# A value product turned round in the attention of a two-layer encoder: f32 probabilities as weights, and another order on TensorE

## The reference

```python
def block(args):                      # one block of 128 queries
    s = einsum('bqhd,bkhd->bhqk', qn_b, k_nope) + einsum('bqhd,bkd->bhqk', qr_b, k_rope)
    p = jax.nn.softmax(s * scale, axis=-1)
    return einsum('bhqk,bkhd->bqhd', p, val)      # 8 heads, val: 64 columns a head
...
mod = (silu(c) @ w_mod[l] + b_mod[l])             # six rows of 1024 a layer and group
h = rmsnorm(x) * (1 + sc1) + sh1
m = concat(rmsnorm(attn), rmsnorm(sgu)) @ w_out   # attn from the blocks above
x = x + ga1 * rmsnorm(m)
h = rmsnorm(x) * (1 + sc2) + sh2
x = x + ga2 * rmsnorm((silu(h @ w_gate) * (h @ w_up)) @ w_down)
```

## Time and profile before

| what | value |
|---|---|
| median of 3 runs | 3696.1 us (3693.67 to 3696.79) |
| the profiled execution's own time | 3700.85 us |
| its span | 3699.0 us |
| mean granted TensorE clock | 0.958 of full speed |
| PE busy | 3358.4 us, 91% of the span, 19532 matmul records |
| DVE, ACT, POOL busy | 1582.8, 1031.7, 1395.8 us |

### The profile page before, as it was taken

One profiled execution on the slowest core, in us unless ns is written; L12 is line 12 of the kernel. 1 busy time (PEld: TensorE's weight loads), 2 busy tenths in 40 slices (PEclk: granted clock), 3 DMA queues, 4 the chain that ended last, 5 costly groups with the idle time before them and its releaser, 6 DMA issues. The chain is left out here.

```text
span 3699.0 us, 48829 instructions
## 1 busy us (share of the span) xinstructions
PE 3358.4 (91%) x19532; PEld 3024.3 (82%) x19532; DVE 1582.8 (43%) x2807; ACT 1031.7 (28%) x2298; POOL 1395.8 (38%) x804
## 2 busy tenths in 40 slices
PE   5997888879899999999998978887989999999996
PEld 1987677767799998889988867776779999899996
DVE  3115677774333333533233146877333333352223
ACT  2323454563300101211004234776330010121001
POOL 2210577740454444545540302000045444455441
PEclk7998899989999999999999989998999999999998
DMA  6204544433322223322223134111232222233221
GB/s 206 70 21 145 150 137 132 155 101 86 115 79 75 75 69 84 113 83 75 80 65 104 58 116 133 27 37 61 75 114 79 76 75 69 83 123 92 80 75 63
DMA packets 397728, 337.90 MB, mean 91 GB/s; under 512 B 107192, under 2 KB 325000, under 8 KB 397504
## 3 DMA queue, kind: packets, MB, share of 16 engines
q1 hardware_dynamic: 249808, 233.18, 20.6%
q10 hardware_dynamic: 147696, 101.61, 9.4%
HBM read 282.87 MB, written 51.87 MB: 90 GB/s over the span
## 5 line engine op out<-in xcount | busy, mean ns | idle before, releaser
L580 POOL TENSOR_SCALAR w_hi<-raw 128x1024 fp32r<-128x1024 f32 (+2 forms) x400 | 436.8, 1092 | 2194.4 <-PE ps L597 2045.4
L582 POOL TENSOR_TENSOR w_lo<-raw,w_hi 128x1024 fp32r<-128x1024 f32 (+2 forms) x400 | 966.7, 2417 | 33.3
L595 PE MATMUL ps<-ht_lo,w_hi 128*128 128x320 f32 x2816 | 874.1, 310 | 5.2 <-DVE ht_lo L1358 3.2
L596 PE MATMUL ps<-ht_hi,w_lo 128*128 128x320 f32 x2816 | 872.2, 310 | 0.0
L597 PE MATMUL ps<-ht_hi,w_hi 128*128 128x320 f32 x2816 | 872.2, 310 | 0.0
L595 PE MATMUL ps<-w_lo,ht_hi 128*128 128x512 f32 (+2 forms) x2040 | 783.8, 384 | 59.4 <-DVE ht_lo L1358 24.3
L596 PE MATMUL ps<-w_hi,ht_lo 128*128 128x512 f32 (+2 forms) x2040 | 777.5, 381 | 0.0
L597 PE MATMUL ps<-w_hi,ht_hi 128*128 128x512 f32 (+2 forms) x2040 | 775.6, 380 | 0.0
L595 PEld LDWEIGHTS ps<-ht_lo,w_hi 128*128 128x128 f32 x2816 | 530.6, 188 | 8.1 <-DVE ht_lo L1358 3.9
L596 PEld LDWEIGHTS ps<-ht_hi,w_lo 128*128 128x128 f32 x2816 | 530.7, 188 | 1.6
L597 PEld LDWEIGHTS ps<-ht_hi,w_hi 128*128 128x128 f32 x2816 | 530.5, 188 | 0.0
(11 more groups left out here) (127 smaller groups left out, 3710.7 us busy)
## 6 DMA issues: line engine op xcount, KB each, us to landing
raw<-in_w_gate_dram SPq DMA_DIRECT2D x88, 512.0 KB, 3.8
raw<-in_w_up_dram SPq DMA_DIRECT2D x88, 512.0 KB, 3.8
raw<-in_w_down_dram SPq DMA_DIRECT2D x88, 512.0 KB, 3.5
raw<-in_w_mod_dram SPq DMA_DIRECT2D x80, 512.0 KB, 4.1
x_rows<-tokm ACTq DMA_DIRECT2D x30, 512.0 KB, 5.0
x_old<-x_rows ACTq DMA_DIRECT2D x30, 512.0 KB, 4.3
kv_rows<-stage ACTq DMA_DIRECT2D x20, 512.0 KB, 3.3
tokm<-kv_rows ACTq DMA_DIRECT2D x30, 320.0 KB, 4.1
```

What stands on the lines that cost most here:

```text
L580: pool.tensor_scalar(hi, r, 1.0, 0.0, ALU.mult, ALU.add).then_inc(s_whi, 1)
L582: pool.tensor_tensor(lo, r, hi.bitcast(F32), ALU.subtract).then_inc(s_w, 1)
L595: pe.matmul(out, lhs[0], rhs[1], start=first, stop=False)
L596: pe.matmul(out, lhs[1], rhs[0], start=False, stop=False)
```

## The change

The value product is turned round: the turned probabilities, now one f32 buffer a unit without hi and lo, are the weights, V in f32 is the moving operand with 64 columns, and the result comes out with queries on the partitions, so nothing is turned back. `probs_hi`, `probs_lo`, `v_hi`, `v_lo`, `values_copy`, `transpose_values`, `low_half` and `invert_sums` go. Of the turned probabilities of a prompt unit ACT copies the first four tiles and DVE the last four; a sample unit is copied by one of them. DVE scales a unit's 64 columns by the inverse of its sum. The buffers `gate_row` and `x_old` hold the turned probabilities during attention. V has two buffers, loaded for two heads at the start.

PE's step is scores of unit n, transposes of unit n-1, value product of unit n-2, with the `prep` transposes between; the loop has two steps beyond the units instead of four. The modulation products stand at every odd step, the last at step 79, at the end of the step, and wait until DVE has read the value product that stands just before them on PE out of bank 6.

```diff
-        def pT(b): return [f[:, 4 * TOK + 2048 * b:...].rearrange("p (k q) -> p k q", q=256) for f in hf]
+        pT = [x.rearrange("p (k q) -> p k q", q=P) for x in (gate_row[:, :], x_old[:, :, :].rearrange("p h c -> p (h c)"))]
...
+        PT_ACT = [s < 2 * NBLK - 1 for s in range(NU)]
+        PT_DVE = [s != 2 * NBLK - 2 for s in range(NU)]
...
-        MOD_WITHIN, MOD_END = {}, {}
...
+        MOD_AT = {2 * i + 1: i for i in range(NLH)}
...
# SP
-                sp.wait_ge(s_vl, 2 * H * (l + 1))
+                sp.wait_ge(s_pv, unit_no(l, H - 1, 0))
                 for t in range(4, NT - 1):
                     sp.dma_start(tokm[:, 1, t, :], sgu_d[t]).then_inc(s_sld[0], 16)
-                sp.wait_ge(s_pt, NPT * H * (l + 1))
+                sp.dma_start(tokm[:, 1, NT - 1, :], sgu_d[NT - 1]).then_inc(s_sld[2], 16)
+                sp.wait_ge(s_pta, act_copies(l + 1, 0, 0))
+                sp.wait_ge(s_ptd, dve_copies(l + 1, 0, 0))
                 for t in range(4):
                     sp.dma_start(tokm[:, 1, t, :], sgu_d[t]).then_inc(s_sld[1], 16)
...
# PE
                     if h or i >= 8:
                         pe.wait_ge(s_htl, transposed[0])
-                        if transposed[1]:
-                            pe.wait_ge(s_od, transposed[1])
...
-                    v = v_prm(h % 2) if k0 == 0 else v_smp
-                    hi, lo = pT(n % 2)
-                    for k in range(part * nk // 2, (part + 1) * nk // 2):
-                        pe.matmul(ps[:, 6, 0:256], v[:, k, :], lo[:, k, :], start=k == 0, stop=False)
-                        ins = pe.matmul(ps[:, 6, 0:256], v[:, k, :], hi[:, k, :], start=False, stop=k == nk - 1)
...
+                    pe.wait_ge(s_pca, act_copies(l, h, s + 1))
+                    pe.wait_ge(s_pcd, dve_copies(l, h, s + 1))
+                    if u:
+                        pe.wait_ge(s_od, u)
+                    if modulated[0]:
+                        pe.wait_ge(s_mrow, modulated[0])
+                    for k in range(nk):
+                        ins = pe.matmul(ps[:, 6, 0:VD], pT[u % 2][:, k, :], v_rows[h % 2][:, k0 + k, :], start=k == 0, stop=k == nk - 1)
...
-                def modulation(i, blocks):
+                def modulation(i, units):
-                    pe.wait_ge(s_ot, blocks)
+                    if units:
+                        pe.wait_ge(s_od, units)
...
-                for n in range(NS + 4):
+                for n in range(NS + 2):
                     if n < NS:
                         scores(*STEPS[n])
+                    if 1 <= n <= NS:
+                        transpose_probs(*STEPS[n - 1])
...
+                    if n >= 2:
+                        values(*STEPS[n - 2])
...
+                    if l == 0 and n in MOD_AT:
+                        modulation(MOD_AT[n], n - 1)
...
# ACT and DVE
+                        act.activation(pT[u % 2][:, 0:w, :], ps[:, 4, 0:w * P].rearrange("p (k q) -> p k q", q=P), ACT.Copy).then_inc(s_pca, 1)
...
+                        dve.tensor_copy(pT[u % 2][:, k0:k0 + w, :], ps[:, 5, 0:w * P].rearrange("p (k q) -> p k q", q=P)).then_inc(s_pcd, 1)
...
+                    link(dve.reciprocal(c, c))
+                    dve.wait_ge(s_pv, u + 1)
+                    dve.tensor_scalar(tokm[:, 0, BLKS[b][2] + i, h * VD:(h + 1) * VD], ps[:, 6, 0:VD], c, None, ALU.mult).then_inc(s_od, 1)
...
-                    link(dve.tensor_tensor(rows, ps[0:2, 6, 256:512], tbank[...], ALU.add))
                     dve.wait_ge(s_ml, i + 1)
-                    dve.tensor_tensor(rows, rows, stage[...], ALU.add).then_inc(s_mrow, 1)
+                    prod = ps[0:2, 6, 256:512]
+                    link(dve.tensor_tensor(prod, prod, tbank[...], ALU.add))
+                    dve.tensor_tensor(rows, prod, stage[...], ALU.add).then_inc(s_mrow, 1)
```

More of the change, by code:

```diff
@@ L333, in trunk_program @@
         NU = len(UNITS)
-        PTB = [-(-BLKS[b][1] // 4) for b, _ in UNITS]
-        NPT = sum(PTB)
+        PT_ACT = [s < 2 * NBLK - 1 for s in range(NU)]
+        PT_DVE = [s != 2 * NBLK - 2 for s in range(NU)]
+        NPA, NPD = sum(PT_ACT), sum(PT_DVE)
         STEPS = [(h, s) for h in range(H) for s in range(NU)]
@@ L418, in trunk_program @@
         s_hl = sem("head_loaded")
-        s_hv = sem("v_loaded")
+        s_hv = [sem(f"v_loaded{i}") for i in range(2)]
         s_prep = sem("head_transposed")
@@ L456, in trunk_program, with unit_no, act_copies, dve_copies @@
         DPP = 2 * HT_
+        def unit_no(l, h, s): return (l * H + h) * NU + s
+        def act_copies(l, h, s):
+            return (l * H + h) * NPA + sum(PT_ACT[:s])
+        def dve_copies(l, h, s): return (l * H + h) * NPD + sum(PT_DVE[:s])
         def after_product(eng, key):
@@ L677, in _ @@
                             ins.then_inc(rdy[b], 1)
[L680 removed]
+                transposed = [l * H * NPREP]
                 def prep(h, i):
@@ L716, in transpose_probs @@
                 def transpose_probs(h, s):
-                    u = (l * H + h) * NU + s
+                    u = unit_no(l, h, s)
                     pe.wait_ge(s_exp, u + 1)
-                    n = (l * H + h) * NPT + sum(PTB[:s])
-                    nk = BLKS[UNITS[s][0]][1]
-                    before = PTB[s - 1] if s else PTB[-1]
-                    for c in range(PTB[s]):
-                        if n:
-                            pe.wait_ge(s_ptl, n - before + 1 if c == 0 and before == 2 else n)
-                        for j in range(min(4, nk)):
-                            ins = pe.transpose(ps[:, 4 + c, j * P:(j + 1) * P], p_buf[u % 2][:, (4 * c + j) * P:(4 * c + j + 1) * P], ident[:, :])
-                        ins.then_inc(s_pt, 1)
@@ L749, in _ @@
-                modulated = [0]
-                def transpose_values(h, b):
-                    n = (l * H + h) * NBLK + b
-                    pe.wait_ge(s_ot, n + 1)
-                    if n:
-                        pe.wait_ge(s_od, n)
-                    pe.wait_ge(s_htl, transposed[0])
-                    transposed[1] += 1
-                    for i in range(2):
-                        ins = pe.transpose(ps[:, 7, o_place(i):o_place(i) + P], ot_buf[n % 2][:, i * P:(i + 1) * P], ident[:, :])
-                    ins.then_inc(s_tr, 1)
@@ L762, in modulation, with four @@
-                def modulation(i, blocks):
+                    w = min(4, BLKS[UNITS[s][0]][1])
+                    def four(bank, k0):
+                        for j in range(w):
+                            ins = pe.transpose(ps[:, bank, j * P:(j + 1) * P], p_buf[u % 2][:, (k0 + j) * P:(k0 + j + 1) * P], ident[:, :])
+                        return ins
+                    if PT_ACT[s]:
+                        if act_copies(l, h, s):
+                            pe.wait_ge(s_pca, act_copies(l, h, s))
+                        four(4, 0).then_inc(s_pta, 1)
@@ L800, in _ @@
                         prep(*prep_at(n, PREP_LATE))
-                    if l == 0 and n in MOD_END:
-                        modulation(MOD_END[n], (n - 2) // 2)
+                    if l == 0 and n in MOD_AT:
+                        modulation(MOD_AT[n], n - 1)
                 def transpose_ffn(key):
@@ L1132, in exponentials @@
                                    scale=SCALE, accum_out=stat[:, 4 + u % 4:5 + u % 4]).then_inc(s_exp, 1)
-                def pt_done(u):
-                    hh, s = divmod(u, NU)
-                    return hh * NPT + sum(PTB[:s + 1])
-                def probs_hi(h, s):
-                    n = ((l * H + h) * NU + s) // 2
-                    u = (l * H + h) * NU + s
-                    nk = BLKS[UNITS[s][0]][1]
-                    if n >= 2 and s % 2 == 0:
-                        act.wait_ge(s_pv, n - 1)
-                    for c in range(PTB[s]):
-                        act.wait_ge(s_pt, pt_done(u) - PTB[s] + c + 1)
-                        w = min(4, nk)
-                        act.activation(pT(n % 2)[0][:, 4 * c:4 * c + w, (s % 2) * P:(s % 2 + 1) * P],
-                                       ps[:, 4 + c, 0:w * P].rearrange("p (k q) -> p k q", q=P), ACT.Copy).then_inc(s_pth, 1)
@@ L1583, in _ @@
                     prep_lo(0, i)
-                for n in range(NS + 4):
+                for n in range(NS + 2):
                     if n < NS:
                         row_max(*STEPS[n])
+                    if 1 <= n <= NS:
+                        probs_copy(*STEPS[n - 1])
                     if prep_at(n, PREP_EARLY):
                         prep_lo(*prep_at(n, PREP_EARLY))
-                    if l == 0 and n in MOD_WITHIN:
-                        modulation_rows(MOD_WITHIN[n])
-                    if n >= 5 and n % 2:
-                        attention_rows(STEPS[n - 5][0], STEPS[n - 5][1] // 2)
-                    if 1 <= n <= NS:
-                        probs_lo(*STEPS[n - 1])
-                    if n >= 2 and n % 2 == 0 and n <= NS:
-                        invert_sums(STEPS[n - 2][0], STEPS[n - 2][1] // 2)
```

(2 more changed lines are left out.)

207 lines of the change are left out of this document (63 added, 144 removed).

## The result

The changed kernel takes 3705.8 us (median of 7 runs, 3703.4 to 3707.6). The kernel before takes 3696.1 in as many runs beside it. The ratio is 1.0025, with an interval of 1.0013 to 1.0037: slower by a quarter of a per cent, where a gain of 3 us was forecast. A second round gave 1.0014 (1.0006 to 1.0023). The profiled execution has a span of 3705.8 us and a granted clock of 0.958, as before.

The account below looks back on a forecast made before the run. PE's queue and waits that the change removes were taken to bound the attention stages. Layer 0 at -9.5 and layer 1 at +6.7 made -2.8 us together, so 3693 from 3696.1, range 3580 to 3770.

Parts of the forecast that it names:

- layer 0's attention: First to last exponential of layer 0: old products, turning back, waits and half clock go, f32 products come; -9.5 us.
- layer 1's attention: First to last exponential of layer 1: old products, turning back and bank 7 waits go, f32 products come; +13.0 us.
- layer 1's tail: Last exponential to output projection in layer 1: the result's way is shorter by two steps, 6.3 us less.
- In layer 0 I book nothing: Layer 0's tail: gating rows land about 15 us after the last scores, about as late as the norm; 0 us.
- there could be a loss of 5: Layer 0's tail: possible loss of 5 us, since the four tiles needed first are issued last.
- The f32 product: Value products on PE: loading the weights binds, 0.11 us a record, 0.22 a product, 119.7 us a layer.
- The difference of the products: PE, each layer: new f32 products at 119.7 us replace fp32r products at 64.5; booked as +55.
- the waits and the clock: Layer 0's attention: 58.0 us of waits for modulation rows go, and 15 us come back from half clock.
- The waits of layer 0: PE's waits for the second addition of the modulation rows in layer 0 all go, 58.0 us.
- rival 3: Layer 0 keeps its waits for modulation rows and its falling clock, 58 + 15 us more, 3766; chance 0.12.
- The new wait of the modulations: Layer 0: each of 40 modulations waits until DVE has read the value product, 0.35 us each, 14 in all.
- Bank 7's waits: Layer 1's attention: PE's waits at bank 7 go, 36.5 us with the part hidden by matmuls.

Follow-up runs that it names:

- e9: Changed kernel with modulation products at odd steps from 1 and at steps 16 and 56, the last at 75 instead of 79: 3694.8 us, 0.9992 of before.
- e6: Changed kernel with SP issuing the gating rows' loads ahead of the last piece of w_out: 3696.3 us, 1.0005 of before.
- e7: Changed kernel with 32 moving columns in layer 0's value product and 128 in layer 1's, instead of 64: 3712.3 us, 1.0047 of before.
- e3: Changed kernel with the two additions of the modulation rows put back as before, both operands of the second in SBUF: 3710.5 us, 1.0035 of before.
- e2: Kernel before with only the modulation rows' additions changed, the second having one operand in PSUM: 3672.1 us, 0.9935 of before.
- e13: Changed kernel with the last modulation product at step 75 and V's load for the second head moved behind the first exponential: 3694.1 us, 0.9990 of before.
- e8: Kernel before with additions through PSUM and odd steps' modulation products ahead of the scores: 3677.7 us, 0.9949 of before.
- e10: Kernel before with additions through PSUM and modulation products at odd steps from 1 and at 16 and 56: 3669.8 us, 0.9925 of before.
- e11: Kernel before with additions through PSUM, modulation products at odd steps from 1 and at 16 and 56, odd steps' ahead of the scores: 3668.9 us, 0.9923 of before.

## Why the prediction was wrong

By two profiles of each kernel, the four stretches that the forecast counted come out like this: layer 0's attention 409.0 to 398.8, -10.2 (forecast -9.5); layer 1's attention 295.1 to 299.7, +4.6 (+13.0); layer 1's tail 23.2 to 19.1, -4.1 (-6.3); layer 0's tail 23.1 to 30.5, +7.4 (0). Together -2.4, where -2.8 was forecast. That agreement is luck: what was booked too high for layer 1's attention, 8.4, stands against what was booked too low for the two tails, 7.4 and 2.2. Outside the four the changed kernel lost 7: 5.5 on the way to layer 1 and 1.8 in the output projection, of which the second is less than the 6.8 by which two profiles of one kernel differ there. So the spans of these profiles moved by +4.9, and the medians by 9.7 and 6.2, where single executions of the changed kernel lie up to 12 us apart.

**The step that failed** is "In layer 0 I book nothing", with "there could be a loss of 5". It was 7.4. The chain that I had named (last modulation, POOL's split, SP's load, gating rows) is there, but it is longer than the "about 15 us after the last scores", and the norm comes earlier than before. The last matmul of the scores in the changed kernel, then the same and the norm in the kernel before:

```profile
796.22 0.28 PE L591 MATMUL ps<-ht_hi 96*128 96x256 f32 x1
```

```profile
807.31 0.28 PE L597 MATMUL ps<-ht_hi 96*128 96x256 f32 x1
...
819.83 1.67 DVE L1615 TENSOR_SCALAR tokm<-tokm,stat 128x512 f32<-128x512 f32 x4
```

DVE was ready to norm 9.3 us after it (12.5 before), and waited for the rows until 20.2 us after it. What I had not put into the step at all is that POOL splits in the tail while DVE norms there: four scalings, which read and write SBUF, took 6.83 us in place of 1.68. The earlier trace rows held the pattern: the additions with both operands in SBUF took 1.24 us on the mean, those with one in PSUM 0.41. In that trace 12 of the 40 began while POOL was in no instruction, and they took 0.41 us too; each of the other 28 ended 0.26 to 0.28 us after the POOL instruction beside which it had begun. e9 takes both, POOL's split and the late rows, out of the tail and gives back 10.7 us there for 1.8 in the attention, and the kernel then stands at 0.9992 of before: the sign that was forecast, with an interval that reaches 1.0000.

The Trainium skill, "SBUF — State Buffer", SBUF: two separate sides, says that DVE (in its two-port modes, or with two inputs in SBUF) and GpSimd take a shared pair of ports as an exclusive lock for a whole instruction. The trace agrees: the two longest of the scalings took 2.55 and 2.56 us and ended 0.28 us behind POOL's subtractions of 2.39 us, and in e6 a scaling of the second four did the same.

**The f32 product.** 0.11 us a record was right, and e7 shows that the moving columns don't set it. The Trainium skill, "TensorE: Matmul & The Clock Gate", LDWEIGHTS (loading the stationary operand), gives 0.107 for 128 columns, an estimate worked out by that page; the rows have 0.112 for each of the two records. The four passes of the Trainium skill, "FP8 and Floating Point Precision", TensorE Precision Notes, would have let the price follow the columns; from 32 to 128 it doesn't, but for a product's first record. That an f32 matmul leaves two records "with unequal weights and moving columns" is not what decides: with 128 of both (e7) it leaves two as well, while a turning of 96 by 128 (`prep`) leaves one.

**The difference of the products** was too large. Summed from start to start, without the idle time behind them, the 530 of 544 records of L744 and L745 that fall in layer 1's attention took 67.7 us before (0.128 each, where I had used 0.1186), and the 1069 of 1088 of L740 114.8 now (0.107 each, where I had used 0.11): +47, not +55. Before, 39 of 77 pieces of a value product began with a record of 0.20 us, so a steady pitch undersold them; now the first record of a prompt unit's product takes 0.06. That is the 8 us by which layer 1 came out better. The same count gives +46 to +47 in layer 0, where the total came out as forecast; so there the waits and the clock gave back some 8 us less than booked, and which of them, no run separates.

**The waits of layer 0** went, and rival 3 with them, for the two reasons that the prediction gave: by e3 the new order alone leaves 4 us of them, by e2 the operands alone leave 30.6. The new wait of the modulations cost 15.8, forecast 14. The granted clock of the stage is 0.98, forecast "near 0.98". Bank 7's waits went as well. The 9.4 us of waits left in layer 1 stood there before with 9.0; those for exponentials rose by 2.2 us there and by 1.7 in layer 0 (forecast 3 each), all at the first unit behind a head's two sample units. Two slips in the prediction's sums change nothing: its 1.8, 0.5 and about 3 for layer 1's tail make 5.3 and not 5.6, and by its own sum gain and loss are equal at 0.111 us a record, not at 0.112.

**Outside the stages** nothing was booked, and this counts for the sign as much as layer 0's tail does: by the profiles, without layer 0's loss the sum would be a gain of 2.5 us, and without the 5.5 on the way to layer 1 one of 0.6. A part is the second load of V on ACT (e13, about 1 us); I had counted PE's instructions and not the DMA that ACT issues ahead of the first exponential. The rest of the 5.5 us stays open. It lies between the end of layer 0's feed-forward and layer 1's first exponential, where the six profiles with the old product show 349.6 to 351.4 us and nine with the new one 351.5 to 357.1. The granted clock there is 0.94 and 0.93 in the two profiles of before, 0.91 and 0.92 in those of the changed kernel; but e2, e8, e10 and e11, at 0.92 with the old product, stay at 351.1 to 351.4. Why the stretch should differ, no run shows.

## What to carry to other kernels

When a change moves the last of the products that others wait for later, follow what waits for it into the next stage, and ask not only what comes late but which engines will now work at the same time. A true f32 product with 128 weight columns cost two records of 0.112 us, whether it streamed 32, 64 or 128 columns: turning a product round so that the long side becomes the weights is paid by their number. One profile of each kernel is too little to place 10 us: a second one moved two stretches by 5 and 7.

## What the runs showed that was not expected

DVE's scaling of 128x512 f32 from SBUF to SBUF takes 0.48 us alone and up to 2.56 us beside POOL's split. An addition of only 2x256 with both operands in SBUF took 1.24 us on the mean and up to 2.59, and ended 0.26 to 0.28 us behind the POOL instruction beside which it had begun; with one operand in PSUM it took 0.41. An f32 matmul with 128x128 weights costs 0.224 us with 32, 64 or 128 moving columns. The same matmuls of an output projection took 143.6 us at a granted clock of 0.95 and 150.4 at 0.91, in two executions of one kernel.
